# Down weights of an expert in one transfer of 4 MB, and the last expert's in freed up buffers

## The chip, the core and the metric

The kernel runs on one core of a Trainium2 chip. The metric is the device time of one execution in microseconds, lower is better; the median of three runs before the change is 1358.1 us (1355.83 to 1360.45).

## The reference

One block of a hybrid decoder on 256 tokens of width 1024, preceded by 16 meta tokens: a Mamba-2 branch and a latent-attention branch, merged by gates, and after them a mixture of 32 experts of which every token uses four. The change touches the loading of the experts' weights alone. What the experts compute:

```python
logits = (tok_x @ w_router + b_router)            # 256 x 32
top_logit, top_e = lax.top_k(logits, 4)
top_w = softmax(top_logit)
# for every expert e, over the tokens that chose it:
hb = x_pad[tok_blk] @ w1[e] + b1[e]               # 1024 -> 2048, "up"
ob = clamped_swiglu(hb) @ w2[e] + b2[e]           # 1024 -> 1024, "down"
y += ob * w_blk                                   # back to the tokens' rows
out = rms_norm(h + y, norm_final)
```

All weights are float32. An expert has 8 MB of up weights and 4 MB of down weights, so the experts read 384 MB from HBM.

## The kernel before

Every engine has a hand-written instruction stream; nothing is scheduled by a planner. The engines meet through counting semaphores. The first third of the time is the two branches; their weights ("slabs") pass through a ring of six slots of 2 MB. From about 412 us on the same ring and parts of a work area hold expert weights.

**Weights in units.** A unit is 2 MB: 128 partitions with a row of 4096 floats (16 KB) each. An expert has four up units and two down units. There are two sets of up buffers, `w1_sb` for even experts (ring slots 3, 4, 5, 0) and `w1_odd` for odd ones, and one set of down buffers, `w2_sb` (slots 2 and 1). Expert 1's first down half comes early, in two pieces of 1 MB, into `extra`.

**Order of the transfers.** All weight transfers are issued by SyncE (SP), in order, each behind a wait until its buffer is free. An issued transfer joins one queue, which the 16 DMA engines serve in order. `load_up(e, t, odd)` issues four units: the first three wait on `up_used`, which TensorE raises after each of the first three pairs of up matmul steps, the last on `up_done`. `load_down(e, t)` issues the first down unit when TensorE has used half of the expert before (`down_used`, raised after k = 3) and the second when it has used all of it (`down_done`). Through a loop over experts 2 to 21 (`TURN = 11`) each step issues `load_up(e + 3)` and then `load_down(e + 1)`. Behind the loop, for e = 22 to 28, the two are in the other order: `load_down(e + 1)` first, then `load_up(e + 3)`. So the loop ends with the down weights of expert 22 and the code behind it begins with those of expert 23. The end is `load_down(30)` and `load_down(31)`.

**TensorE.** A step handles expert t's end and expert t+1's beginning: `up(t + 1)` (up bias, then eight k of four matmuls; between them transposes of t's activations, the scatter of t-1 and the gather of t+2), then `down(t)` (eight k of two matmuls). `down` waits for the first down unit before k = 0 and for the second before k = 4. A 32-bit matmul stands in the trace as two instructions. The last step has no gather; `down(30)` has transposes between k = 3 and k = 4, and `down(31)` has the scatter of expert 30 there. After it come the last scatter, the final norm and the store.

The semaphore count needed in a wait grows with the number of transfers that were made into a buffer; an overflow round for experts with more than 64 tokens has its own loop and isn't entered with these inputs.

Of the kernel before, what the change touches and what calls it, by code (L numbers as in the profile page):

```python
# [27 lines left out]
P = 128  # L28
D = 1024
# [16 lines left out]
E = 32  # L46
# [28 lines left out]
NSLOT, SLOT = 6, 4096  # L75
# [5 lines left out]
UNIT = 4096  # L81
W1_UNITS, W2_UNITS = 4, 2
E_UNITS = W1_UNITS + W2_UNITS
W1_SLOT = [3, 4, 5, 0]
W2_SLOT = [2, 1]
ODD_AT = [25736, 13824, 20480, 7168]
EXTRA_AT = [0, 11264]

# [14 lines left out]
def meta_ssd_mla_moe(nc, x, meta, slabs, vecs, rows, wts, b1, b2, out):  # L103
    ctx = ExitStack()
    with ctx:
# [17 lines left out]
        ring = sb("ring", NSLOT * SLOT)  # L123
# [92 lines left out]
        actT = w(4096, 512).rearrange("p (j t) -> p j t", j=4)  # L216
# [6 lines left out]
        actT_last = xgT  # L223
# [34 lines left out]
        def sem(name):  # L258
            return ctx.enter_context(nc.semaphore(name))
# [8 lines left out]
        w2_in = [sem(f"w2_in{i}") for i in range(W2_UNITS)]  # L268
        extra_in = [sem(f"extra_in{i}") for i in range(len(EXTRA_AT))]
        up_used, down_used = sem("up_used"), sem("down_used")  # L270
# [34 lines left out]
        down_done, ob_ready, scattered = sem("down_done"), sem("ob_ready"), sem("scattered")  # L305
# [35 lines left out]

        w1_sb = [ring[:, s * SLOT:s * SLOT + UNIT] for s in W1_SLOT]
        w1_odd = [w(at, UNIT) for at in ODD_AT]
        w2_sb = [ring[:, s * SLOT:s * SLOT + UNIT] for s in W2_SLOT]
# [17 lines left out]
        def _(sp):  # L362
# [6 lines left out]
            def unit_of(e, u):  # L369
                return wts[bass.ds((e * E_UNITS + u) * P, P), :]  # L370
# [2 lines left out]
                buf, arrival = (w1_odd, w1_odd_in) if odd else (w1_sb, w1_in)  # L373
                sp.dma_start(buf[u], unit_of(e, u)).then_inc(arrival[u], 16)

            def load_w2(e, c):
                sp.dma_start(w2_sb[c], unit_of(e, W1_UNITS + c)).then_inc(w2_in[c], 16)

            def load_extra(i):
                half = unit_of(1, W1_UNITS)[:, i * (UNIT // 2):(i + 1) * (UNIT // 2)]  # L380
# [36 lines left out]

            def load_down(e, t):

                sp.wait_ge(down_used, t)  # L420
                load_w2(e, 0)
                sp.wait_ge(down_done, t)
                load_w2(e, 1)

            sp.wait_ge(*used["so3"])
            load_w1(0, 3, False)
# [6 lines left out]
            load_w1(1, 2, True)  # L433
            load_extra(1)
            sp.wait_ge(*used["wout0"])
            load_w2(0, 0)
            sp.wait_ge(*used["wout1"])
            load_w2(0, 1)
            sp.wait_ge(xn_ready, 4)
            sp.wait_ge(h1_squared, 4)  # L440
            sp.wait_ge(h1_kept, 1)
# [2 lines left out]
            load_up(2, 2, 0)  # L444
            load_up(3, 3, 1)
            sp.wait_ge(down_done, 1)
            load_w2(1, 1)
            load_w2(2, 0)
            load_up(4, 4, 0)
            sp.wait_ge(down_done, 2)  # L450
            load_w2(2, 1)
            with sp.Fori(1, TURN) as i:
                for odd in (0, 1):
                    e = 2 * i + odd
# [3 lines left out]
                load_down(e + 1, e + 1)  # L458
                load_up(e + 3, e + 3, (e + 1) % 2)
            load_down(E - 2, E - 2)  # L460
            load_down(E - 1, E - 1)
            sp.wait_ge(count_ready, 1)
            cm = sp.value_load(cmax_i[0:1, 0:1], min_val=0, max_val=SEQ)
            with sp.If(cm > SLOTS):
                with sp.Fori(1, SEQ // SLOTS) as r:
# [880 lines left out]
        def _(pe):  # L1346
# [24 lines left out]
            for i in range(6):  # L1371
                b, k0 = ORDER[i // 2], 4 * (i % 2)
                n = BLOCKS[b][1]
# [348 lines left out]
            def up(t, pair, odd, between):  # L1722

                pe.wait_ge(xgT_ready, t + 1)
                weights, arrival = (w1_odd, w1_odd_in) if odd else (w1_sb, w1_in)
                for k in range(KD):
                    between(k)
                    if k % 2 == 0:
                        pe.wait_ge(arrival[k // 2], 16 * (pair + 1))
# [10 lines left out]
            def down(t, to=6, actT=actT, between=None, first=None):  # L1740

                halves = [w2_sb[0][:, 0:UNIT // 2], w2_sb[0][:, UNIT // 2:UNIT], w2_sb[1][:, 0:UNIT // 2], w2_sb[1][:, UNIT // 2:UNIT]]
                if first == 1:
                    halves[0:2] = extra
                pe.wait_ge(actT_ready, t + 1)
                if between is None:
                    pe.wait_ge(scat_ready, t + 1)
                for k in range(KD):
                    if between is not None and k == 4:
                        between()  # L1750
                    if k == 4:
                        pe.wait_ge(w2_in[1], 16 * (t + 1))
                    elif first == 1 and k in (0, 2):
                        pe.wait_ge(extra_in[k // 2], 16)
                    elif k == 0:
                        pe.wait_ge(w2_in[0], 16 if first == 0 else 16 * t)
                    for j in range(2):
                        at = k % 2 * 1024 + j * 512
                        last = mm(bank[to][j * SLOTS:(j + 1) * SLOTS, :], actT[:, k % 4, (k // 4) * SLOTS:(k // 4 + 1) * SLOTS],
                                  halves[k // 2][:, at:at + 512], k == 0, k == KD - 1)  # L1760
                    if k == 3:
                        last.then_inc(down_used, 1)
                last.then_inc(down_done, 1)

            def expert_round(r):
                t0, pair0 = r * E, r * (E // 2)

                def step(t, pair, odd, gathers, scatters, routing, first=None):
                    def between(k):
                        if k == 2:  # L1770
                            act_transposes(t)
                        elif k == 4:
                            if scatters:
                                scatter(t - 1, scat_last if t is t0 else scat)
                            hot_transposes(t)
                            if routing:
                                weights_trans()
                        elif k == 6 and gathers:
                            pe.wait_ge(actT_ready, t + 1)
                            if routing:  # L1780
                                pe.wait_ge(wT_ready, 1)
# [4 lines left out]
                    up(t + 1, pair, odd, between)  # L1786
                    if gathers:
                        gather_trans(t + 2)
                    if routing:
                        down_bias()  # L1790
                    if gathers:
                        down(t, first=first)
                    else:
                        pe.wait_ge(scat_ready, t + 1)
                        down(t, between=lambda: last_transposes(t + 1))

                def first_between(k):
                    if k == 6:
# [2 lines left out]
                def last_transposes(t):  # L1801
                    act_transposes(t)
                    pe.wait_ge(up_read, t + 1)
                    hot_transposes(t, 5)
# [8 lines left out]
                    pe.wait_ge(count_ready, 1)  # L1813
                up_bias(t0)
                gather_trans(t0)
                up(t0, pair0, 0, first_between)
# [15 lines left out]
                down(t0 + E - 1, 4, actT_last, lambda: scatter(t0 + E - 2))  # L1832

            FIRST = 0
            pe.wait_ge(xn_scaled, 2)
# [35 lines left out]
def pack_experts(inp):  # L1871

    import numpy as np
    up = inp["w_mlp1"][0].reshape(E, W1_UNITS, 2, P, 2, 512, 2).transpose(0, 1, 3, 2, 4, 6, 5).reshape(E, W1_UNITS, P, UNIT)
    down = inp["w_mlp2"][0].reshape(E, W2_UNITS, 4, P, D).transpose(0, 1, 3, 2, 4).reshape(E, W2_UNITS, P, UNIT)
    return np.concatenate([up, down], axis=1).reshape(E * E_UNITS * P, UNIT)


# [48 lines left out]
```

## Time and profile before

| | |
|---|---|
| median of 3 runs | 1358.1 us (1355.83 to 1360.45) |
| profiled execution | 1358.35 us, span 1356.6 us |
| granted TensorE clock, mean | 0.997 |
| TensorE busy | 1304.2 us, 96% of the span |
| DMA queue of SP | 460.63 MB in 33424 packets, 81.5% of 16 engines' span |
| chain that ended last | PE 61%, DMA 29%, issue 4% |

The span is what the profiler sees between the first and the last instruction; the profiled execution took 1.75 us more. The share of busy time doesn't say which of TensorE and the DMA engines sets the time: both are at over 90% through the experts. That is read from the stretches in which one of them waits.

### The profile page before, as it was taken

To read this page: it belongs to the slowest core of one execution; us is meant where nothing else is said; L and a number is where in the kernel's file an instruction comes from. 1 tells how busy PE (TensorE), PEld (TensorE's weight loads), DVE (VectorE), ACT (ScalarE), POOL (GpSimd) and SP (SyncE) were. 2 spreads that over 40 slices of the span, in tenths; PEclk is the share of its full clock that TensorE was granted. 3 is DMA by queue.
4 is the path that set the end of the run, shared out by engine and by line. 5 is a ranking of instruction groups with operands and counts; after the bars stand their busy time and mean duration, and the time that the engine had idled before them with its cause. 6 is when DMAs were issued, how large, how long until landed. Compare 5 with 4: busy or idle time off the path is not lost.

```text
span 1356.6 us, 17927 instructions
## 1 busy us (share of the span) xinstructions
PE 1304.2 (96%) x7105; PEld 638.0 (47%) x7105; DVE 459.3 (34%) x1129; ACT 320.4 (24%) x649; POOL 66.7 (5%) x74
## 2 busy tenths in 40 slices
PE   7999999999999999999999999999999999999995
PEld 5858888899974333333333322333333333333331
DVE  4838889988534211112111211111121111211111
ACT  3636767755411111011101101100110010111011
POOL 0000004422103000000000000000000000000000
PEclk9999999999999999999999999999999999999998
DMA  6431334244878999999999999999999999999994
GB/s 238 148 124 64 125 125 168 107 162 187 337 289 323 422 403 426 429 428 430 427 430 427 429 429 428 429 427 430 428 429 429 428 386 424 431 427 429 428 426 164
DMA packets 33763, 461.85 MB, mean 340 GB/s; under 512 B 3808, under 2 KB 3808, under 8 KB 5552
## 3 DMA queue, kind: packets, MB, share of 16 engines
q1 hardware_dynamic: 33424, 460.63, 81.5%
q8 instruction: 34, 0.56, 0.2%
q10 hardware_dynamic: 288, 0.52, 0.1%
q14 instruction: 17, 0.14, 0.0%
HBM read 460.09 MB, written 1.05 MB: 340 GB/s over the span
## 4 chain that ended last, share of the span: by engine, by line
PE 61%; DMA 29%; issue 4%; POOL 3%; DVE 2%; ACT 1%; SPq 0%; POOLq 0%; DVEq 0%; ACTq 0%
PE bank L1348 58%; DMA ring<-wts_dram 29%; POOL work L517 1%; POOL work L514 1%; PE bank L1690 1%; PE bank L1696 1%; DMA ring<-slabs_dram 1%; DVE split L913 0%; PE bank L1712 0%; PE bank L1479 0%; DVE work L847 0%; DVE work L846 0%; DVE work L845 0%; ACT split L559 0%; PE bank L1499 0%
## 5 line engine op out<-in xcount | busy, mean ns | idle before, releaser
L1348 PE MATMUL bank<-ring,work 128*64 128x512 f32 (+5 forms) x2248 | 541.7, 592 | 29.1 <-DMA ring<-wts_dram 28.1
L1348 PE MATMUL bank<-work 128*64 128x512 f32 (+8 forms) x2216 | 434.0, 546 | 3.2 <-DVE work L1267 1.0
L1348 PEld LDWEIGHTS bank<-ring,work 128*64 128x64 f32 (+2 forms) x2248 | 179.1, 142 | 340.4 <-issue 292.9
L1348 PEld LDWEIGHTS bank<-work 128*64 128x64 f32 (+4 forms) x2216 | 146.5, 143 | 258.8 <-issue 246.8
L1348 PE MATMUL bank<-hn_hi,split 128*128 128x256 f32 (+1 forms) x896 | 173.0, 288 | 1.4 <-DVE split L913 1.3
L1296 DVE COPY work<-bank 128x256 f32<-128x256 f32 x31 | 13.2, 425 | 473.8 <-PE bank L1712 473.8
L1348 PEld LDWEIGHTS bank<-hn_hi,split 128*128 128x128 f32 x896 | 141.4, 189 | 3.4 <-issue 1.9
L1348 PE MATMUL bank<-hn_lo,split 128*128 128x256 f32 (+1 forms) x448 | 127.2, 284 | 0.0
L1271 DVE TENSOR_SCALAR work<-bank 128x512 f32<-128x512 f32 x32 | 22.1, 692 | 273.4 <-PE bank L1348 273.4
L913 DVE TENSOR_TENSOR split<-ring,split 128x1024 fp32r<-128x1024 f32 x80 | 100.0, 1253 | 27.1 <-ACT split L559 26.8
L756 ACT ACTIVATE work<-bank 128x512 f32<-128x512 f32 x32 | 19.1, 598 | 328.3 <-PE bank L1348 324.2
L559 ACT ACTIVATE split<-ring 128x1024 fp32r<-128x1024 f32 x80 | 84.1, 1054 | 36.2 <-PE bank L1348 36.0
L1348 PEld LDWEIGHTS bank<-hn_lo,split 128*128 128x128 f32 x448 | 84.4, 188 | 0.2
L776 ACT ACTIVATE work<-bank 128x512 f32<-128x512 f32 x32 | 19.1, 597 | 223.5 <-PE bank L1348 223.5
L771 ACT ACTIVATE work<-bank 128x512 f32<-128x512 f32 x32 | 19.1, 597 | 146.8 <-PE bank L1696 146.8
L1348 PE MATMUL bank<-y_hi,split 128*128 128x256 f32 x256 | 46.2, 283 | 0.0
L760 ACT ACTIVATE work<-bank 128x512 f32<-128x512 f32 x32 | 19.1, 597 | 106.9 <-PE bank L1690 106.9
L1348 PEld LDWEIGHTS bank<-y_hi,split 128*128 128x128 f32 x256 | 40.0, 192 | 0.0
L1348 PE MATMUL bank<-y_lo,split 128*128 128x256 f32 x128 | 36.2, 283 | 0.0
L514 POOL TENSOR_SCALAR work<-work 128x256 f32<-128x256 f32 x16 | 14.1, 884 | 237.5 <-ACT work L701 237.5
L1696 PEld LDWEIGHTS bank<-shifted,work 128*128 128x128 f32 x128 | 13.4, 140 | 26.0 <-issue 26.0
L1690 PEld LDWEIGHTS bank<-shifted,work 128*128 128x128 f32 x128 | 13.4, 140 | 26.0 <-issue 25.2
(247 smaller groups left out, 899.9 us busy)
## 6 DMA issues: line engine op xcount, KB each, us to landing
ring<-wts_dram SPq DMA_DIRECT2D x127, 2048.0 KB, 24.2
work<-wts_dram SPq DMA_DIRECT2D x64, 2048.0 KB, 25.3
ring<-slabs_dram SPq DMA_DIRECT2D x23, 2048.0 KB, 7.5
ring<-slabs_dram SPq DMA_DIRECT2D x2, 1152.0 KB, 5.2
work<-wts_dram SPq DMA_DIRECT2D x2, 1024.0 KB, 19.8
work<-x_dram SPq DMA_DIRECT2D x3, 512.0 KB, 11.5
ring<-slabs_dram SPq DMA_DIRECT2D x1, 1536.0 KB, 12.0
ring<-slabs_dram SPq DMA_DIRECT2D x1, 1280.0 KB, 8.7
```

The lines of the kernel that those rows point to most:

```text
L514: link(pool.tensor_scalar(ztanh[:, c % 2, :], ztanh[:, c % 2, :], 1.0, None, ALU.add))
L517: pool.tensor_tensor(zw, ztanh[:, c % 2, :], zcopy[:, c % 2, :], ALU.mult).then_inc(zw_ready, 1)
L559: a.activation(split[p % NSPLIT][:, 0], piece(p), ACT.Copy).then_inc(hi_ready, 1)
L756: a.activation(xg[:, :], bank[7][:, :], ACT.Copy).then_inc(xg_ready, 1)
L760: a.activation(xgT[:, :, :].rearrange("p j t -> p (j t)"), bank[7][:, :], ACT.Copy).then_inc(xgT_ready, 1)
L771: a.activation(actT[:, :, :].rearrange("p j t -> p (j t)"), bank[7][:, :], ACT.Copy, scale=0.5).then_inc(actT_ready, 1)
L776: a.activation(ob[:, :], bank[at][:, :], ACT.Copy).then_inc(ob_ready, 1)
L913: d.tensor_tensor(split[p % NSPLIT][:, 1], piece(p), split[p % NSPLIT][:, 0], ALU.subtract).then_inc(lo_ready, 1)
L1271: d.tensor_scalar(glu[:, :], bank[4][:, :], LIMIT, None, ALU.min).then_inc(glu_ready, 1)
L1348: return pe.matmul(o, lhsT, rhs, start=start, stop=stop)
L1690: last = pe.transpose(bank[7][:, j * P:(j + 1) * P], xg[:, j * P:(j + 1) * P], ident[:, :])
L1696: last = pe.transpose(bank[7][:, j * P:(j + 1) * P], act[:, j * P:(j + 1) * P], ident[:, :])
```

## The change

The two down units of an expert become one transfer: `w2_sb` is now one buffer of 8192 columns over ring slots 1 and 2, the weights lie in HBM with 32 KB in a row for each partition, and `load_down` waits for `down_done` alone and issues 4 MB. `down_used` is gone. `down` waits for the whole 4 MB before k = 0. Experts 0 and 1 still get halves (expert 0 both, expert 1 the second; its first comes into `extra` as before). Experts 2 to 30, 29 of them, get the 4 MB transfer.

The last expert's down weights don't go to `w2_sb`: its first 2 MB go to `w1_sb[0]` and the rest, as 1 MB, 512 KB and 512 KB, to `w1_sb[1]`. Expert 30's up weights were there, and the waits are for `up_used` of expert 30. `down(31)` waits for the pieces before k = 0, 4, 6 and 7. The order of the loop and of the code behind it is the same as before.

```diff
-W2_SLOT = [2, 1]
+W2_SLOT = 1
...
-            def load_w2(e, c):
-                sp.dma_start(w2_sb[c], unit_of(e, W1_UNITS + c)).then_inc(w2_in[c], 16)
+            wide = wts.rearrange("(a b) n -> a (b n)", b=2)
+            def w2_of(e):
+                return wide[bass.ds((e * (E_UNITS // 2) + W1_UNITS // 2) * P, P), :]
+            def load_w2_half(e, c):
+                sp.dma_start(w2_sb[:, c * UNIT:(c + 1) * UNIT], w2_of(e)[:, c * UNIT:(c + 1) * UNIT]).then_inc(w2_in, 16)
...
             def load_down(e, t):
-                sp.wait_ge(down_used, t)
-                load_w2(e, 0)
                 sp.wait_ge(down_done, t)
-                load_w2(e, 1)
+                sp.dma_start(w2_sb, w2_of(e)).then_inc(w2_in, 16)
...
             sp.wait_ge(down_done, 1)
-            load_w2(1, 1)
-            load_w2(2, 0)
+            load_w2_half(1, 1)
             load_up(4, 4, 0)
-            sp.wait_ge(down_done, 2)
-            load_w2(2, 1)
+            load_down(2, 2)
...
             load_down(E - 2, E - 2)
-            load_down(E - 1, E - 1)
+            sp.wait_ge(up_used, (E - 2) * (W1_UNITS - 1) + 1)
+            sp.dma_start(w1_sb[0], w2_of(E - 1)[:, 0:UNIT]).then_inc(w1_in[0], 16)
+            sp.wait_ge(up_used, (E - 2) * (W1_UNITS - 1) + 2)
+            for at, n, arrival in ((0, 2048, w1_in[1]), (2048, 1024, extra_in[0]), (3072, 1024, extra_in[1])):
+                sp.dma_start(w1_sb[1][:, at:at + n], w2_of(E - 1)[:, UNIT + at:UNIT + at + n]).then_inc(arrival, 16)
...
-                    if k == 4:
-                        pe.wait_ge(w2_in[1], 16 * (t + 1))
+                    if final and k in (0, 4):
+                        pe.wait_ge(w1_in[k // 4], 16 * (E // 2 + 1))
+                    elif final and k >= 6:
+                        pe.wait_ge(extra_in[k - 6], 32)
                     elif first == 1 and k in (0, 2):
                         pe.wait_ge(extra_in[k // 2], 16)
-                    elif k == 0:
-                        pe.wait_ge(w2_in[0], 16 if first == 0 else 16 * t)
+                    elif first == 1 and k == 4:
+                        pe.wait_ge(w2_in, 48)
+                    elif k == 0 and not final:
+                        pe.wait_ge(w2_in, 32 if first == 0 else 16 * (t + 1) if later else 16 * (t + 2))
...
-                    if k == 3:
-                        last.then_inc(down_used, 1)
                 last.then_inc(down_done, 1)
```

On SP, where the loop ends and the code behind it begins (`COMPARE_AND_BRANCH` closes the loop), before:

```order
L377 ISA [waits down_used]
L377 DMA ring<-wts_dram 128x4096
L377 ISA [waits down_done]
L377 DMA ring<-wts_dram 128x4096
L452 REGISTER_ALU
L452 COMPARE_AND_BRANCH
L377 DMA ring<-wts_dram 128x4096 [waits down_used]
L377 DMA ring<-wts_dram 128x4096 [waits down_done]
L374 DMA work<-wts_dram 128x4096 [waits up_used] x3
L374 DMA work<-wts_dram 128x4096 [waits up_done]
```

The same place now:

```order
L426 ISA [waits down_done]
L426 DMA ring<-wts_dram 128x8192
L453 REGISTER_ALU
L453 COMPARE_AND_BRANCH
L426 DMA ring<-wts_dram 128x8192 [waits down_done]
L374 DMA work<-wts_dram 128x4096 [waits up_used] x3
L374 DMA work<-wts_dram 128x4096 [waits up_done]
```

Expert 22's transfer and expert 23's still stand next to each other, and the second now waits for the end of `down(22)` instead of its middle. The end of SP's weights, before:

```order
L374 DMA work<-wts_dram 128x4096 [waits up_done]
L377 DMA ring<-wts_dram 128x4096 [waits down_used]
L377 DMA ring<-wts_dram 128x4096 [waits down_done]
L377 DMA ring<-wts_dram 128x4096 [waits down_used]
L377 DMA ring<-wts_dram 128x4096 [waits down_done]
```

The same place now:

```order
L374 DMA work<-wts_dram 128x4096 [waits up_done]
L426 DMA ring<-wts_dram 128x8192 [waits down_done]
L463 DMA ring<-wts_dram 128x4096 [waits up_used]
L466 DMA ring<-wts_dram 128x2048 [waits up_used]
L466 DMA ring<-wts_dram 128x1024 x2
```

The last expert's pieces no longer wait for `down(30)`.

## Rows read from the trace of the kernel before

**Rows 1.** The page: the span, TensorE, the chain by engine, issues of weights.
```profile
span 1356.6 us, 17927 instructions
PE 1304.2 (96%) x7105; PEld 638.0 (47%) x7105; DVE 459.3 (34%) x1129; ACT 320.4 (24%) x649; POOL 66.7 (5%) x74
...
PE 61%; DMA 29%; issue 4%; POOL 3%; DVE 2%; ACT 1%; SPq 0%; POOLq 0%; DVEq 0%; ACTq 0%
...
ring<-wts_dram SPq DMA_DIRECT2D x127, 2048.0 KB, 24.2
```

**Rows 2.** Windows: stretch, length, busy by engine, TensorE clock, DMA share, GB/s.
```profile
550.00:700.00 150.00, 150.00 (x718) 49.44 (x714) 25.84 (x71) 16.76 (x29) 0.00 (x0) 1.00 1.01 429
700.00:1100.00 400.00, 378.78 (x1784) 123.76 (x1776) 57.34 (x157) 39.11 (x68) 0.00 (x0) 1.00 1.01 428
1100.00:1105.00 5.00, 4.46 (x22) 1.68 (x20) 3.95 (x11) 1.11 (x2) 0.00 (x0) 1.00 0.79 338
1105.00:1110.00 5.00, 3.88 (x22) 1.25 (x24) 0.00 (x0) 0.07 (x1) 0.00 (x0) 1.00 0.80 269
1110.00:1115.00 5.00, 5.00 (x28) 1.50 (x23) 0.00 (x0) 0.53 (x1) 0.00 (x0) 1.00 0.99 400
1115.00:1120.00 5.00, 5.00 (x25) 1.75 (x24) 0.00 (x0) 0.60 (x1) 0.00 (x0) 1.00 1.00 423
1120.00:1290.00 170.00, 170.00 (x808) 56.09 (x806) 26.69 (x73) 17.44 (x30) 0.00 (x0) 1.00 1.01 428
```

**Rows 3.** Chain of waits: start, us, what. A DMA piece runs from issue to landing.
```profile
757.67 25.47 DMA ring<-wts_dram
783.19 3.68 PE bank L1348 x16
787.04 25.48 DMA ring<-wts_dram
...
1080.73 25.45 DMA ring<-wts_dram
1106.23 8.26 PE bank L1348 x40
...
1130.26 11.62 PE bank L1348 x56
...
1157.66 11.62 PE bank L1348 x56
...
1298.28 22.77 DMA ring<-wts_dram
```

**Rows 4.** SP's issues in time: start, us from first to last, count.
```profile
480.31 0.81 SPq L377 DMA_DIRECT2D ring<-wts_dram  x2
484.91 15.52 SPq L374 DMA_DIRECT2D ring<-wts_dram  x4
507.70 0.33 SPq L377 DMA_DIRECT2D ring<-wts_dram  x1
...
1080.73 29.53 SPq L377 DMA_DIRECT2D ring<-wts_dram  x3
```

**Rows 5.** The issue at 500.1 us and its landing.
```profile
L374 SPq DMA_DIRECT2D ring<-wts_dram x1: 328/328/328, 500.1 to 500.1; - x1
...
DMA to landing us min/median/max: 13.6/13.6/13.6
```

**Rows 6.** The issue at 1105.1 us and its landing.
```profile
L377 SPq DMA_DIRECT2D ring<-wts_dram x1: 342/342/342, 1105.1 to 1105.1; - x1
...
DMA to landing us min/median/max: 7.7/7.7/7.7
```

**Rows 7.** DMA packets in 1040 to 1100 us (rows of 16 KB).
```profile
DMA packets 1771, 25.71 MB, mean 428 GB/s; under 512 B 202, under 2 KB 202, under 8 KB 202
...
q1 hardware_dynamic: 1771, 25.71, 100.7%
```

**Rows 8.** DMA packets in 353 to 354.5 us (rows of 8 KB).
```profile
DMA packets 78, 0.64 MB, mean 426 GB/s; under 512 B 1, under 2 KB 1, under 8 KB 1
...
q1 hardware_dynamic: 78, 0.64, 102.1%
```

**Rows 9.** Timeline of TensorE near the end: start, us, what, [idle before].
```profile
1294.58 7.09 PE L1348 MATMUL bank<-ring,work 128*64 128x512 f32 x32
...
1321.19 3.65 PE L1348 MATMUL bank<-ring,work 128*64 128x512 f32 x16 [1.33 <-DMA ring<-wts_dram]
...
1325.96 3.65 PE L1348 MATMUL bank<-ring,work 128*64 128x512 f32 x16 [0.32 <-DMA ring<-wts_dram]
...
1333.16 5.35 PE L1348 MATMUL bank<-ring,work 128*64 128x512 f32 x16 [3.54 <-DMA ring<-wts_dram]
...
1338.44 1.99 PE L1348 MATMUL bank<-work 64*128 64x512 f32 x8
...
1340.36 3.65 PE L1348 MATMUL bank<-ring,work 128*64 128x512 f32 x16
```

**Rows 10.** Windows at the end, columns as in rows 2.
```profile
1330.00:1333.00 3.00, 0.00 (x0) 0.00 (x0) 0.00 (x0) 0.26 (x1) 0.00 (x0) 1.00 0.98 385
1333.00:1338.00 5.00, 4.84 (x16) 1.78 (x16) 0.00 (x0) 0.00 (x0) 0.00 (x0) 0.66 0.78 319
```

More of the change, by code:

```diff
@@ L267, in meta_ssd_mla_moe @@
         w1_odd_in = [sem(f"w1_odd_in{i}") for i in range(W1_UNITS)]
-        w2_in = [sem(f"w2_in{i}") for i in range(W2_UNITS)]
+        w2_in = sem("w2_in")
         extra_in = [sem(f"extra_in{i}") for i in range(len(EXTRA_AT))]
-        up_used, down_used = sem("up_used"), sem("down_used")
+        up_used = sem("up_used")
         pool_step, dve_step, act_step = sem("pool_step"), sem("dve_step"), sem("act_step")
@@ L343, in meta_ssd_mla_moe @@
         w1_odd = [w(at, UNIT) for at in ODD_AT]
-        w2_sb = [ring[:, s * SLOT:s * SLOT + UNIT] for s in W2_SLOT]
+        w2_sb = ring[:, W2_SLOT * SLOT:W2_SLOT * SLOT + 2 * UNIT]
         extra = [w(at, UNIT // 2) for at in EXTRA_AT]
@@ L374, in load_w1 @@
                 sp.dma_start(buf[u], unit_of(e, u)).then_inc(arrival[u], 16)
[L376 to L377 removed]
+            wide = wts.rearrange("(a b) n -> a (b n)", b=2)
[3 more added lines that the diff above has]
+                sp.dma_start(w2_sb[:, c * UNIT:(c + 1) * UNIT], w2_of(e)[:, c * UNIT:(c + 1) * UNIT]).then_inc(w2_in, 16)
             def load_extra(i):
[L380 removed]
+                half = w2_of(1)[:, i * (UNIT // 2):(i + 1) * (UNIT // 2)]
                 sp.dma_start(extra[i], half).then_inc(extra_in[i], 16)
@@ L435, in _ @@
             sp.wait_ge(*used["wout0"])
-            load_w2(0, 0)
+            load_w2_half(0, 1)
             sp.wait_ge(*used["wout1"])
-            load_w2(0, 1)
+            load_w2_half(0, 0)
             sp.wait_ge(xn_ready, 4)
@@ L464, in _ @@
             with sp.If(cm > SLOTS):
+                sp.wait_ge(down_done, E)
                 with sp.Fori(1, SEQ // SLOTS) as r:
@@ L1720, in up_bias, with up @@
                            b1all[i * E:(i + 1) * E, j * 512:(j + 1) * 512], True, False)
-            def up(t, pair, odd, between):
+            def up(t, pair, odd, between, later=False):
                 pe.wait_ge(xgT_ready, t + 1)
@@ L1728, in up @@
                     if k % 2 == 0:
-                        pe.wait_ge(arrival[k // 2], 16 * (pair + 1))
+                        extra_use = 1 if later and not odd and k < 4 else 0
+                        pe.wait_ge(arrival[k // 2], 16 * (pair + 1 + extra_use))
                     for i in range(2):
@@ L1738, in up, with down @@
                 last.then_inc(up_done, 1)
-            def down(t, to=6, actT=actT, between=None, first=None):
-                halves = [w2_sb[0][:, 0:UNIT // 2], w2_sb[0][:, UNIT // 2:UNIT], w2_sb[1][:, 0:UNIT // 2], w2_sb[1][:, UNIT // 2:UNIT]]
+            def down(t, to=6, actT=actT, between=None, first=None, later=False, final=False):
+                halves = [w2_sb[:, i * (UNIT // 2):(i + 1) * (UNIT // 2)] for i in range(4)]
                 if first == 1:
                     halves[0:2] = extra
+                if final:
+                    halves = [w1_sb[0][:, 0:UNIT // 2], w1_sb[0][:, UNIT // 2:UNIT], w1_sb[1][:, 0:UNIT // 2], w1_sb[1][:, UNIT // 2:UNIT]]
                 pe.wait_ge(actT_ready, t + 1)
@@ L1785, in step @@
                     up_bias(t + 1)
-                    up(t + 1, pair, odd, between)
+                    up(t + 1, pair, odd, between, later=r is not FIRST)
                     if gathers:
@@ L1791, in step @@
                     if gathers:
-                        down(t, first=first)
+                        down(t, first=first, later=r is not FIRST)
                     else:
                         pe.wait_ge(scat_ready, t + 1)
-                        down(t, between=lambda: last_transposes(t + 1))
+                        down(t, between=lambda: last_transposes(t + 1), later=r is not FIRST)
                 def first_between(k):
@@ L1815, in expert_round @@
                 gather_trans(t0)
-                up(t0, pair0, 0, first_between)
+                up(t0, pair0, 0, first_between, r is not FIRST)
                 gather_trans(t0 + 1)
@@ L1831, in expert_round @@
                 pe.wait_ge(up_read, t0 + E)
-                down(t0 + E - 1, 4, actT_last, lambda: scatter(t0 + E - 2))
+                down(t0 + E - 1, 4, actT_last, lambda: scatter(t0 + E - 2), later=r is not FIRST, final=r is FIRST)
             FIRST = 0
@@ L1874, in pack_experts @@
     up = inp["w_mlp1"][0].reshape(E, W1_UNITS, 2, P, 2, 512, 2).transpose(0, 1, 3, 2, 4, 6, 5).reshape(E, W1_UNITS, P, UNIT)
-    down = inp["w_mlp2"][0].reshape(E, W2_UNITS, 4, P, D).transpose(0, 1, 3, 2, 4).reshape(E, W2_UNITS, P, UNIT)
+    down = inp["w_mlp2"][0].reshape(E, 8, P, D).transpose(0, 2, 1, 3).reshape(E, W2_UNITS, P, UNIT)
     return np.concatenate([up, down], axis=1).reshape(E * E_UNITS * P, UNIT)
```

## The prediction, made blind

> **What bounds the kernel now.** I read the page first [rows 1]. TensorE is busy 96% of the span, yet 29% of the chain is DMA; both are near their limit, so the share decides nothing. The windows by stage split it [rows 2]. From 550 to 700 us TensorE has no idle time; from 700 to 1100 us it lacks 21 us (400 less 378.78); from 1120 to 1290 us it has none again. The DMA engines move 428 to 429 GB/s in all three. The reader is to see that the queue of weights is the steady side and that TensorE only now and then feels it.
>
> The chain gives both periods [rows 3]. From 757.67 to 787.04 us is one expert while the weights bind: 29.37 us for six units, 4.89 us for 2 MB. From 1130.26 to 1157.66 us is one expert while TensorE binds: 27.40 us. Every expert thus costs the queue 1.97 us more than TensorE. TensorE runs ahead on data loaded earlier until that lead is used up, and then it follows the queue. At the end it follows the queue: the chain there is a transfer issued at 1298.28 us. So the end of the kernel is the time at which the queue has delivered its last units, plus a tail, and any microsecond in which the queue is empty counts in full, if TensorE catches up later. The experts left after a break decide that.
>
> One break stands in the windows [rows 2]. Against 429 GB/s, the four windows from 1100 to 1120 us lose 5 x (1 - 338/429) = 1.06, 1.86, 0.34 and 0.07 us, 3.3 us together. This is where the loop of SP ends: expert 23's first down unit waits there for the middle of `down(22)`, and the freed up buffers stand behind it. The last unit of expert 22 lands at 1080.73 + 25.45 = 1106.2 us, and the next one was issued at 1105.1 us and took 7.7 us to land [rows 3, 6]. A unit itself takes 4.9 us, so an empty queue costs 2.8 us from issue to first effect.
>
> **The change part by part.**
>
> Fewer and longer packets. In 1040 to 1100 us, 1569 data packets (1771 less 202 small ones) take 100.7% of 16 engines for 60 us, 616 ns each for 16 KB [rows 7]. Packets of 8 KB take 24.5/77 = 318 ns [rows 8]. A cost that does not grow with bytes is then 2 x 318 - 616 = 20 ns at most; this is an estimate from two short windows. An engine has 8 such packets less in each of 29 transfers: at 20 ns that is 160 ns each, 4.6 us in all. The other end is 0, if the hardware cuts the 32 KB row in two. I take 2.3 us, the middle: -2.3 (0 to -4.6).
>
> The loading rule of thumb would give far more. The Trainium skill (SBUF — State Buffer, "The DMA setup-cost knee") says that each transfer pays about 2 us that doesn't scale with bytes and that one should use the largest transfer possible. By that the sum would get 29 x 2 = 58 us back. The rows disagree here: the six transfers of an expert take 29.37 us for 12 MB at 429 GB/s, with no room for six such costs; they are paid beside one another in a full queue.
>
> The start. Before, expert 2's down units were issued at 480.7 us (the first) and at 507.70 us (the second) [rows 4]. Now both go at 507.70 us. The last up unit ahead of it was issued at 484.91 + 15.19 = 500.1 us and landed at 513.7 us [rows 4, 5]; with one unit less ahead it lands at 508.8 us. The 4 MB issued at 507.70 us to a nearly empty queue lands at 507.7 + 7.7 + 4.9 = 520.3 us instead of 508.8 + 9.8 = 518.6 us: +1.7 (1 to 3; the upper end adds half of a start again). TensorE doesn't feel it, but the queue is later by that from there on.
>
> The steady loop. The 4 MB is issued at `down_done` and TensorE must have it whole before k = 0. The period is 29.3 us; `down` takes 7.2 us, so the transfer has 22.1 us from issue to landing, of which 9.8 are its own: some 12 us of up units are still ahead of it, and the queue does not run empty. TensorE's two waits per expert become one of 1.9 us. Cost: 0, hidden behind the queue.
>
> Where the loop ends. SP issues expert 22's 4 MB and then waits with expert 23's until `down(22)` has ended, while the four free up buffers stand behind it. The queue ends with expert 22's landing; TensorE then takes 7.1 us for 32 matmul instructions [rows 9] and 0.1 to signal; then come 2.8 us of start and 9.8 us of transfer. Landing to landing is 19.8 us instead of 9.8, a hole of 10.0 us. The 3.3 us of before go: +6.7. If the clock falls during TensorE's wait, `down(22)` is 1.7 us longer. Range 6.2 to 9.
>
> Is the hole paid back? Between it and the landing of expert 30's down weights lie 44 units, 215 us of queue. TensorE needs 7 x 27.40 us to the end of `down(29)` and 18.2 us for the last up (1301.7 to 1319.9 us [rows 9]). The hole delays TensorE's own line by 3.7 us (the end of `down(22)` goes from 1109.9 us, when the third issue of the group at 1080.73 that waits for it goes [rows 4], to 1106.2 + 1.7 - 1.5 + 7.2 = 1113.6 us, 1.5 being the 20 shorter transfers until then); from there it would be ready for `down(30)` at 1113.6 + 191.8 + 18.2 = 1323.6 us. The queue delivers at 1325.9 + 1.7 + 6.7 - 2.3 = 1332.0 us. The queue binds again two experts before the end, so the hole counts in full.
>
> The end. Before, from the landing of expert 30's second unit (1325.9 us) to the end of the last matmul of `down(31)` (1344.0) there are 18.1 us, with a wait of 3.54 us for expert 31's weights and 5.35 us for 16 instructions that otherwise take 3.65 [rows 9]. Now expert 31's pieces lie directly behind expert 30's 4 MB, all landed 9.8 us after it, before TensorE asks for the second. That wait goes. What is late next is `down(30)`: both its halves now stand behind the landing. The tail is 3.65 + 1.2 + 3.65 for it, then 3.65 + 2.0 + 3.65, 17.8 us, and before it TensorE waits 4.1 us (it is ready 7.2 + 18.0 us after the landing of expert 29's, the next lands 29.3 us after it). Idle for 3.54 us before, TensorE had a granted clock of 0.66 over 1333 to 1338 us against 1.00 [rows 10], part of it at 1.2 instead of 2.4 GHz, and lost 1.7 us. I take the same loss: 19.5 against 18.1, +1.4 (-0.3 without it, +3 with a longer one). Removed instructions on SP and TensorE cost nothing: SP waits for buffers all the time.
>
> **Sum.** -2.3 + 1.7 + 6.7 + 1.4 = +7.5 us. The profiled execution goes from 1358.35 to 1365.9 us; it lies 0.25 us above the median, so the forecast is 1358.1 + 7.5 = 1365.6 us. Low ends together: -4.6 + 1.0 + 6.2 - 0.3 = +2.3, 1360.4. High ends, not all at once: about +13, 1371.
>
> **The rivals.**
>
> Wide rows move faster (the other side). If the 4 MB landed in 9.3 instead of 9.8 us, 29 of them would give 14.5 us instead of 2.3: 1353.4 us. The sum turns to zero at 0.26 us more per transfer than I counted, 2.7% of it. For it speaks only that no 32 KB packet is in the trace; against it that the whole cost per packet is 20 of 616 ns. 0.05.
>
> Every transfer pays its start. If the 2.8 us stood in the stream for each, 29 fewer would give 81 us, more than TensorE can follow: its waits after 700 us are 21.2 + 0.5 + 1.1 + 5.2 = 28 us [rows 2, 9], so the time would be 1330 us. A full queue at 4.89 us per unit speaks against it. 0.01. By the Trainium skill's 58 us it would be the same 1330, since that too is more than the waits.
>
> The low ends meet (no clock loss at the end, packets at 20 ns): +2.3 to +4.1, at 1361.5 us, no change that can be measured. 0.13.
>
> Rows are cut in two (the change doesn't do what it says): the 2.3 us don't come, 1367.9 us. For it: nothing in the trace shows a packet over 16 KB. 0.13.
>
> The clock falls in every joined wait of 1.9 us. Waits up to 1.33 us kept it, 3.54 did not [rows 9]. TensorE's period becomes 27.4 + 1.7 = 29.1 us, still under 29.3; only the hole grows: 1367.3 us. 0.10.
>
> **How the numbers follow.** The forecast has the remaining 0.58. A measurement can tell about 0.3%, 4.1 us, so slower begins at 1362.2 us. Slower: 0.58 + 0.13 + 0.10 = 0.81; the same: 0.13; faster: 0.06. The range is 1359.5 to 1371: below are the faster cases, above what several high ends would add.
>
> **What would show it.** The windows around the end of SP's loop: a hole of 10 us in the DMA engines' work, with SP waiting for `down_done` and the issue some 7 us behind the landing. A packet count lower by 29 x 144, and the period of an expert at 29.3 us while the weights bind. One wait of TensorE per expert of about 1.9 us. In the last 35 us no hole in the queue, a wait of about 4 us before `down(30)` and none before `down(31)`. I am wrong if the period falls below 29.1 us, if TensorE never waits after 1120 us, or if the hole is shorter than 8 us.

## The result and the profile after

The changed kernel takes 1365.38 us (median of 5 runs, 1364.91 to 1365.98) against 1358.1 us, now the median of five executions of the kernel before: a ratio of 1.0051, 95% interval 1.0038 to 1.0063. It is slower by 7.3 us where 7.5 were forecast. The profiled execution took 1365.08 us with a span of 1363.3 us, 6.7 us more than before. Five more executions later gave 1364.51 us against 1358.28 us for the kernel before beside them, 6.2 us slower. Medians of the kernel before lie between 1357.4 and 1358.7 us from set to set, so the cost of the change is known to about 1 us: 6 to 7.5 us.

The page of the kernel after, the same lines as in [rows 1]:

```profile
span 1363.3 us, 17847 instructions
PE 1308.6 (96%) x7105; PEld 640.2 (47%) x7105; DVE 459.1 (34%) x1129; ACT 320.3 (23%) x649; POOL 66.6 (5%) x74
...
DMA packets 29875, 461.84 MB, mean 339 GB/s; under 512 B 3376, under 2 KB 3376, under 8 KB 5376
...
PE 58%; DMA 32%; issue 4%; POOL 3%; DVE 2%; ACT 1%; SPq 0%; POOLq 0%; DVEq 0%; ACTq 0%
...
ring<-wts_dram SPq DMA_DIRECT2D x29, 4096.0 KB, 20.9
```

There are 29 transfers of 4 MB, and 3888 packets fewer than the 33763 of before: 29 x 144 less the 288 of two more pieces for the last expert. So the rows of 32 KB are moved in one packet each; had they been cut, only the small packets would be fewer. The trace's records of single packets say the same: 3712 of them, 29 x 128, have 32768 bytes.

The windows that answer to [rows 2] (stretch, length, busy by engine, TensorE clock, DMA share, GB/s):

```profile
700.00:1100.00 400.00, 381.35 (x1776) 124.77 (x1774) 57.27 (x157) 38.99 (x67) 0.00 (x0) 0.98 1.01 430
...
1105.00:1110.00 5.00, 4.89 (x26) 1.77 (x24) 2.57 (x5) 1.12 (x2) 0.00 (x0) 1.00 0.11 46
1110.00:1115.00 5.00, 5.00 (x24) 1.44 (x20) 1.39 (x7) 0.00 (x0) 0.00 (x0) 1.00 0.00 0
1115.00:1120.00 5.00, 5.00 (x29) 1.60 (x28) 0.00 (x0) 0.60 (x1) 0.00 (x0) 1.00 0.85 308
1120.00:1290.00 170.00, 168.40 (x801) 55.50 (x800) 26.23 (x72) 18.05 (x31) 0.00 (x0) 1.00 1.00 429
```

The reader is to see the DMA column: from 1105 to 1115 us the engines move next to nothing, where before they were at 269 and 400 GB/s. TensorE is fully busy over the same 10 us, so a look at TensorE alone would not find the hole. It does wait again before 1290 us (168.40 of 170), which it did not before.

The chain of waits, start, us and what (compare [rows 3]):

```profile
1027.45 21.98 DMA ring<-wts_dram
1049.47 7.11 PE bank L1354 x32
1056.75 21.98 DMA ring<-wts_dram
...
1087.74 20.26 DMA ring<-wts_dram
1108.05 11.69 PE bank L1354 x56
...
1252.16 21.89 DMA ring<-wts_dram
1274.10 7.11 PE bank L1354 x32
1281.23 23.09 DMA ring<-wts_dram
1304.45 8.80 PE bank L1354 x32
1313.26 20.31 DMA ring<-wts_dram
1333.71 3.65 PE bank L1354 x16
```

The period is now 1056.75 - 1027.45 = 29.30 us, with the whole `down` (7.11 us) behind the landing. Less four up units of 4.89 us each, that leaves 9.7 us for a 4 MB transfer in a full queue. From 1252 us on the chain is the queue again.

SP's issues around the end of its loop, and the landing of the issue at 1115.2 us:

```profile
1087.74 27.77 SPq L426 DMA_DIRECT2D ring<-wts_dram  x2
1115.57 2.06 SPq L374 DMA_DIRECT2D work<-wts_dram  x4
...
DMA to landing us min/median/max: 12.4/12.4/12.4
```

Expert 22's 4 MB landed at 1087.74 + 20.26 = 1108.0 us, expert 23's was issued at 1115.2 and landed at 1127.6: 19.6 us from landing to landing, 9.9 more than a 4 MB transfer takes in a full queue (9.7). Before, the two units of expert 23 landed 13.0 us behind expert 22's (the second issued at 1109.9 us, 9.3 us to land).

TensorE at the end (answers to [rows 9]):

```profile
1304.45 8.78 PE L1354 MATMUL bank<-ring,work 128*64 128x512 f32 x32 [2.88 <-DMA ring<-wts_dram]
...
1333.71 3.65 PE L1354 MATMUL bank<-ring,work 128*64 128x512 f32 x16 [2.40 <-DMA ring<-wts_dram]
...
1338.10 7.09 PE L1354 MATMUL bank<-ring,work 128*64 128x512 f32 x32
...
1347.03 3.65 PE L1354 MATMUL bank<-ring,work 128*64 128x512 f32 x16
```

`down(31)` has no wait any more: the second half of `down(30)` and the first of `down(31)` stand in one row of 32 instructions.

### The profile page after: what moved, and what is told of

Its sections match the earlier page's. It is cut to its first block, busy times and chain, and to the rows that moved or that the text cites. A ratio compares the mean times of both kernels' runs of the same rounds, so it can differ in the third digit from the quotient of the medians.

```text
span 1363.3 us, 17847 instructions
## 1 busy us (share of the span) xinstructions
PE 1308.6 (96%) x7105; PEld 640.2 (47%) x7105; DVE 459.1 (34%) x1129; ACT 320.3 (23%) x649; POOL 66.6 (5%) x74
## 4 chain that ended last, share of the span: by engine, by line
PE 58%; DMA 32%; issue 4%; POOL 3%; DVE 2%; ACT 1%; SPq 0%; POOLq 0%; DVEq 0%; ACTq 0%
PE bank L1354 56%; DMA ring<-wts_dram 32%; POOL work L523 1%; POOL work L520 1%; DMA ring<-slabs_dram 1%; PE bank L1696 1%; PE bank L1702 1%; DVE split L919 0%; PE bank L1485 0%; PE bank L1718 0%; DVE work L853 0%; DVE work L852 0%; DVE work L851 0%; ACT split L565 0%; PE bank L1505 0%
## 5 line engine op out<-in xcount | busy, mean ns | idle before, releaser
L919 DVE TENSOR_TENSOR split<-ring,split 128x1024 fp32r<-128x1024 f32 x80 | 100.0, 1252 | 27.1 <-ACT split L565 26.8
```

The costliest lines, as they stand in the source:

```text
L919: d.tensor_tensor(split[p % NSPLIT][:, 1], piece(p), split[p % NSPLIT][:, 0], ALU.subtract).then_inc(lo_ready, 1)
```

## The experiments

All times are medians: of five executions for most kernels, of six for the last expert's weights in the kernel before, of eleven for each of the two kernels with the order turned in three steps, of four for the second run of the 16 KB kernel. Each of the three sets ran beside the kernel before on the same chip, which gave 1358.7, 1357.4 and 1358.3 us. The changed kernel is called "the change" below. It was timed with the result (1365.38 us) and in the third set (1364.51 us), but not in the first two, so a difference to it from these carries about 1 us of doubt between sets.

**Rows of 16 KB in the 4 MB transfer.** One transfer as in the change, but the weights lie in units as before.

```diff
             def w2_of(e):
-                return wide[bass.ds((e * (E_UNITS // 2) + W1_UNITS // 2) * P, P), :]
+                return wts[bass.ds((e * E_UNITS + W1_UNITS) * P, 2 * P), :].rearrange("(c p) n -> p c n", c=2)
...
-                sp.dma_start(w2_sb, w2_of(e)).then_inc(w2_in, 16)
+                sp.dma_start(w2_pair, w2_of(e)).then_inc(w2_in, 16)
```

> The changed kernel with one edit: the down weights lie in HBM in rows of 16 KB again, and the single 4 MB transfer takes two such rows per partition. Same waits, same number of transfers. Theory (the cost is per packet): the 4 MB takes 2 x 4.89 = 9.79 us from landing to landing instead of 9.71, 29 times, +2.3 us on 1365.4, 1367.7. Rival (what was saved came from having fewer transfers and semaphore writes): 1365.4. A second rival (wide rows are read better by HBM, hidden so far behind something): over 1370.

Measured: 1369.81 us, ratio to before 1.0081 (1.0067 to 1.0095), 4.4 us over the change. Two transfers of its chain, with the weights binding:

```profile
1028.47 22.04 DMA ring<-wts_dram
...
1059.54 20.33 DMA ring<-wts_dram
```

They land at 1050.51 and 1079.87 us, 29.36 us apart, which is the period of the kernel before. The number of transfers is that of the change, so the gain in the period (29.30 us) is by packets, and the rival that fewer transfers save something is out. But 4.4 us are more than the packets explain, so it ran again beside the change.

> The changed kernel once more, beside the next two on the same chip: 1365.4, within 0.8.

> The kernel of e1_rows_16k (rows of 16 KB in the 4 MB transfer) again. The first time it was 4.4 us slower than the changed kernel where the packets explain 2.3; its trace has TensorE at half clock for 2.8 us before down(30), behind a wait of 4.21 us. Theory (both belong to it: 2.3 of packets and about 2 of the clock, which falls at another place since the waits are longer): 4 to 4.5 us over the changed kernel. Rival (the clock's part was chance): 2.3 over it.

Measured: the change 1364.51 us, the 16 KB kernel 1370.52 us: 6.0 us apart, more than the theory's 4 to 4.5, and the rival of 2.3 is out. The rows of the first run show where more than 2.3 us come from. Its weights for expert 30 land 1.9 us later than those of the change (1335.5 against 1333.6), which is the packets' part. Then TensorE at the end (timeline) and the windows there:

```profile
1335.64 6.46 PE L1355 MATMUL bank<-ring,work 128*64 128x512 f32 x16 [4.21 <-DMA ring<-wts_dram]
```

```profile
1335.00:1342.00 7.00, 6.36 (x16) 1.91 (x16) 0.01 (x1) 0.00 (x0) 0.00 (x0) 0.55 0.98 413
```

The 16 instructions take 6.46 us instead of 3.65, with a granted clock of 0.55 in the 7 us, mostly at the lower of the two levels (1.2 against 2.4 GHz). That is 2.8 us on the path, 4.7 together. The trace of the second run has the clock fall at two places that count, `down(22)` (chain) and `down(30)` (timeline):

```profile
1108.67 13.38 PE bank L1355 x56
...
1336.73 5.35 PE L1355 MATMUL bank<-ring,work 128*64 128x512 f32 x16 [2.58 <-DMA ring<-wts_dram]
```

The 56 instructions that begin with `down(22)` take 11.69 us in the trace of the change beside it. The 1.7 us more delay the issue of expert 23's weights into an empty queue, and 1.7 us more are lost in `down(30)`; with 2 us of packets that is 5.4 us, and the spans differ by 5.2 (1368.0 and 1362.8 us). Wide rows thus save about 2 us by packets, as forecast. The loss of clock on the path came on top in both traces of the 16 KB kernel, 2.8 and 3.4 us, at different places; why this kernel loses it and the change doesn't is not shown.

**The up units first, the last expert's pieces before expert 30's.**

```diff
+                load_up(e + 3, e + 3, (e + 1) % 2)
                 load_down(e + 1, e + 1)
-                load_up(e + 3, e + 3, (e + 1) % 2)
-            load_down(E - 2, E - 2)
...
+            load_down(E - 2, E - 2)
```

> The changed kernel with the order behind SP's loop as in the loop (the up units of e + 3 first, then the down weights of e + 1) and the last expert's pieces ahead of expert 30's 4 MB. No two down transfers stand next to each other, so the hole of 10 us near 1110 us goes. Theory A, as the prediction put it (each empty microsecond of the queue counts in full): 1355.5. Theory B (the order at the end counts too: the down weights of expert 29 come four units later in the queue, 19.6 us, less the hole of 9.9; from their landing TensorE has 7.2 + 18.2 + 8.4 + 9.3 = 43.1 us of work left, against 17.1 behind expert 30's): landing of expert 29's at 1304.3 + 9.7 = 1314.0, last matmul at 1357.1 instead of 1350.7, 1371.8. I expect B.

Measured: 1370.29 us, ratio 1.0080 (1.0066 to 1.0094), 4.9 us slower than the change though the hole is gone. Theory A falls. TensorE at its end:

```profile
1313.55 7.09 PE L1354 MATMUL bank<-ring,work 128*64 128x512 f32 x32 [0.23 <-DMA ring<-wts_dram]
...
1342.88 7.09 PE L1354 MATMUL bank<-ring,work 128*64 128x512 f32 x32
...
1351.82 3.65 PE L1354 MATMUL bank<-ring,work 128*64 128x512 f32 x16
```

Expert 29's weights come at 1313.4 us instead of 1304.3, and behind them TensorE has no wait until the end of `down(31)` at 1355.5 us, 4.8 us later than in the change. B holds; it put that end at 1357.1 us, 1.6 too late: the landing came 0.6 us earlier, and the work behind it took 42.1 us and not 43.1.

**The hole alone: the order turned in three steps.**

```diff
+                ahead = (2, 2, 2, 1, 1, 1, 0)[e - 2 * TURN]
+                load_up(e + 3, e + 3, (e + 1) % 2, range(ahead))
                 load_down(e + 1, e + 1)
-                load_up(e + 3, e + 3, (e + 1) % 2)
+                load_up(e + 3, e + 3, (e + 1) % 2, range(ahead, W1_UNITS))
```

> The changed kernel with the order of transfers turned in three steps instead of one: behind SP's loop, 2, 2, 2, 1, 1, 1 and 0 of the four up units of e + 3 go ahead of the down weights of e + 1, the rest behind it, so that the end has the same order as before and the queue always has up units in it while SP waits for down_done. Theory (the hole of 9.9 us counts in full when the order at the end stays): expert 30's weights land at 1333.6 - 9.9 = 1323.7, last matmul at 1340.8, 1355.5; up to 2.8 more if the clock falls before down(30). Rival (TensorE binds behind the old hole, so that only its own delay of 3.7 us comes back): 1361.7.

Measured: 1355.08 us, ratio 0.9984 (0.9975 to 0.9993). That is 2.3 us under the kernel before beside it, and 10.3 us under the change. The change ran in other sets; measured each against the kernel before beside it, the two lie 8.5 to 9.6 us apart, and their spans 10.0 to 10.5. The hole's 9.9 us thus come back whole or nearly so, and the rival of 1361.7 us is out. The windows across the old hole, and SP's issues:

```profile
1105.00:1110.00 5.00, 4.87 (x24) 1.76 (x24) 3.95 (x11) 1.11 (x2) 0.00 (x0) 1.00 1.00 426
1110.00:1115.00 5.00, 5.00 (x28) 1.41 (x26) 0.00 (x0) 0.60 (x1) 0.00 (x0) 1.00 1.08 413
1115.00:1120.00 5.00, 5.00 (x26) 1.77 (x24) 0.00 (x0) 0.60 (x1) 0.00 (x0) 1.00 0.92 387
```

```profile
1085.77 0.33 SPq L426 DMA_DIRECT2D ring<-wts_dram  x1
1090.23 4.51 SPq L374 DMA_DIRECT2D work<-wts_dram  x2
1113.22 0.33 SPq L426 DMA_DIRECT2D ring<-wts_dram  x1
```

Expert 23's 4 MB is still issued 7.2 us behind expert 22's landing. The wait of SP is the same; two up units in the queue cover it. So what the merge costs at this place is the hole and not the wait. Behind 1106 us TensorE waits once for weights, before `down(30)`:

```profile
1323.24 3.65 PE L1356 MATMUL bank<-ring,work 128*64 128x512 f32 x16 [0.19 <-DMA ring<-wts_dram]
```

Its own work and the queue thus reach the end nearly together; a queue that is faster still would give no more than that 0.19 us.

**The same with expert 30's weights in two halves.**

```diff
-            load_down(E - 2, E - 2)
+            sp.wait_ge(down_done, E - 2)
+            for c in range(2):
+                sp.dma_start(w2_sb[:, c * UNIT:(c + 1) * UNIT], w2_of(E - 2)[:, c * UNIT:(c + 1) * UNIT]).then_inc(extra_in[c], 16)
```

> As e6_gradual, and expert 30's down weights as two transfers of 2 MB with a wait each, expert 31's as two of 2 MB. Theory: down(30) begins with the first half, 4.9 us earlier, until TensorE's own line binds (43.1 us behind the landing of expert 29's weights at 1294.4: 1337.5 against 1340.8): 1352.2. Rival (the wait before down(30) isn't on the path once the hole is gone): the same as e6_gradual.

Measured: 1355.70 us, ratio 0.9987 (0.9978 to 0.9996), no gain over 1355.08. The rival holds: the wait taken away was only the 0.19 us above, and TensorE's own work of 27.4 us per expert sets the end. My figure of 1337.5 us for TensorE's line began at the landing of expert 29's weights, put at 1294.4 us, but in the trace of the kernel with whole transfers TensorE comes to `down(29)` only at 1297.9 us and finds them there.

**One part of the change alone: the last expert's weights, in the kernel before.** TensorE's waits for them are changed as in the change.

```diff
             load_down(E - 2, E - 2)
-            load_down(E - 1, E - 1)
+            sp.wait_ge(up_used, (E - 2) * (W1_UNITS - 1) + 1)
+            sp.dma_start(w1_sb[0], unit_of(E - 1, W1_UNITS)).then_inc(w1_in[0], 16)
+            sp.wait_ge(up_used, (E - 2) * (W1_UNITS - 1) + 2)
+            for at, n, arrival in ((0, 2048, w1_in[1]), (2048, 1024, extra_in[0]), (3072, 1024, extra_in[1])):
+                sp.dma_start(w1_sb[1][:, at:at + n], unit_of(E - 1, W1_UNITS + 1)[:, at:at + n]).then_inc(arrival, 16)
...
```

> The kernel before with one part of the change alone: expert 31's down weights go into the up buffers of expert 30, in pieces, and don't wait for down(30). Units of 2 MB, two waits and the order stay. Theory: the wait of 3.54 us before down(31) and the 1.7 us at half clock behind it go, and nothing else: 1358.1 - 5.2 = 1352.9. Rival (TensorE meets the weights of expert 30 anyway, so nothing is won, as the tail of the changed kernel with its gain of only 1 us suggests): 1357.

Measured: 1354.94 us, ratio 0.9967 (0.9955 to 0.9979): 3.7 us faster. Its timeline of TensorE:

```profile
1322.02 3.65 PE L1353 MATMUL bank<-ring,work 128*64 128x512 f32 x16 [1.31 <-DMA ring<-wts_dram]
...
1326.82 3.65 PE L1353 MATMUL bank<-ring,work 128*64 128x512 f32 x16 [0.34 <-DMA ring<-wts_dram]
1331.87 3.65 PE L1353 MATMUL bank<-ring,work 128*64 128x512 f32 x16 [1.39 <-DMA ring<-wts_dram]
```

The wait of 3.54 us is not gone but 1.39 us long, since the first piece of 2 MB needs its 4.9 us behind expert 30's unit; the slow stretch behind it is gone. This part of the change is a gain by itself.

**The other part alone: the merge, in the changed kernel.**

```diff
-            sp.wait_ge(up_used, (E - 2) * (W1_UNITS - 1) + 1)
-            sp.dma_start(w1_sb[0], w2_of(E - 1)[:, 0:UNIT]).then_inc(w1_in[0], 16)
...
+            load_down(E - 1, E - 1)
...
```

> The changed kernel without the last part: expert 31's down weights are a 4 MB transfer into the down buffer, issued when down(30) has ended. Theory: issue at 1333.7 + 8.4 = 1342.1, landing 2.8 + 9.8 us later at 1354.8, a wait of 12.6 us and 1.7 us of half clock before down(31), last matmul at 1365.8 instead of 1350.7: +15, 1380.5. Rival (the queue's start is hidden and down(30) ends earlier than I think): +10, 1375.

Measured: 1380.55 us, ratio 1.0160 (1.0146 to 1.0174), 15.2 us over the change. The merge alone costs 21.9 us over the kernel before beside it; most of that is a wait before `down(31)`:

```profile
1353.59 5.47 PE L1350 MATMUL bank<-ring,work 128*64 128x512 f32 x16 [12.58 <-DMA ring<-wts_dram]
```

**Expert 2's weights in halves, in the changed kernel.**

```diff
             load_w2_half(1, 1)
+            sp.dma_start(w2_sb[:, 0:UNIT], w2_of(2)[:, 0:UNIT]).then_inc(early_in, 16)
             load_up(4, 4, 0)
-            load_down(2, 2)
+            sp.wait_ge(down_done, 2)
+            load_w2_half(2, 1)
```

> The changed kernel with expert 2's down weights in two halves as before the change, the first issued when down(1) ... that is when down(0) has ended, the second when down(1) has, and the wait for both before k = 0. Theory: the queue's short break near 510 us goes (measured 2.2 us later than in the kernel before by then) and everything behind it comes earlier by that: 1363.2. Rival (a lead lost so early is bought back before the queue binds): 1365.4.

> The kernel of e8_start (expert 2's down weights in halves) again. Its trace showed the break of 2.3 us at 507 us gone and another of 2.5 us at 535 us in its place, behind the first 4 MB transfer, with 0.5 us left over. Theory: 0.5 us under the changed kernel. Rival (the full 2.2 us): 1363.2.

Measured: 1364.20 us, and 1363.78 us beside 1364.51 for the change: 0.7 us, within the scatter. Two windows, first of the change, then of this kernel:

```profile
510.00:515.00 5.00, 5.00 (x26) 1.76 (x24) 0.00 (x0) 0.60 (x1) 0.00 (x0) 1.00 0.73 315
...
535.00:540.00 5.00, 5.00 (x28) 1.38 (x26) 0.00 (x0) 0.60 (x1) 0.00 (x0) 1.00 1.09 469
```

```profile
510.00:515.00 5.00, 5.00 (x26) 1.77 (x24) 0.00 (x0) 0.60 (x1) 0.00 (x0) 1.00 1.01 426
...
535.00:540.00 5.00, 5.00 (x30) 1.68 (x24) 0.00 (x0) 0.42 (x2) 0.00 (x0) 1.00 0.93 347
```

The break moves from expert 2's 4 MB to expert 3's. In both kernels the first 4 MB that waits for `down_done` meets a nearly empty queue. The start term is a cost of the merge and isn't removed by this one exception.

**A version that beats both.** Units of 2 MB and two waits per expert as before, the last expert's weights in the up buffers in four pieces of 1 MB, and one up unit ahead of the down weights for e = 22 to 24.

```diff
+                ahead = (1, 1, 1, 0, 0, 0, 0)[e - 2 * TURN]
+                load_up(e + 3, e + 3, (e + 1) % 2, range(ahead))
                 load_down(e + 1, e + 1)
...
+            sp.wait_ge(up_used, (E - 2) * (W1_UNITS - 1) + 1)
+            for i, arrival in ((0, w1_in[0]), (1, extra_in[0])):
+                sp.dma_start(w1_sb[0][:, i * 2048:(i + 1) * 2048], unit_of(E - 1, W1_UNITS)[:, i * 2048:(i + 1) * 2048]).then_inc(arrival, 16)
...
```

> The kernel before (2 MB units of 16 KB rows, two waits per expert) with expert 31's down weights in the up buffers of expert 30 as four pieces of 1 MB, and one up unit ahead of the down weights for e = 22 to 24, so that the queue has work while SP waits for the middle of down(22). Theory: 3.9 us for the last expert, as in e4_before_last_only, 1.4 for the shorter first piece (the wait of 1.39 us before down(31) goes), 3.4 for the hole: 1358.7 - 8.7 = 1350.0. Rival (the hole of before is not on the path): 1353.4.

Measured: 1350.80 us, ratio 0.9951 (0.9938 to 0.9965), 6.6 us faster than the kernel before beside it, where the theory gave 8.7. The part for the last expert alone had given 3.7, so the shorter piece and the filled hole together gave some 2.8 (each kernel beside the kernel before of its set) and not 4.8. The timeline of the kernel with that part alone says why: its waits before `down(30)` and `down(31)` are 1.31, 0.34 and 1.39 us, 3.0 together, and behind them TensorE's own work is the limit. The issues around the end of the loop:

```profile
1085.78 0.34 SPq L374 DMA_DIRECT2D work<-wts_dram  x1
1105.75 5.14 SPq L377 DMA_DIRECT2D ring<-wts_dram  x2
```

It beats the change with its hole repaired (1355.08) by 4.3 us, by 3.0 in the spans of the two traces. Both are bound by TensorE behind 1110 us, so what counts is when `down(22)` ends: at 1110.5 us here and at 1113.2 us there, because a whole `down` lies behind the landing of one 4 MB transfer, and half of one behind a unit's. That is 2.7 us of the 3.0; the rest of the 4.3 is not explained.

## Why the prediction was right

The forecast, +7.5 us, and its terms against the two traces (span +6.7):

| Step | forecast, us | measured, us | read from |
|---|---|---|---|
| fewer packets | -2.3 | -2.0 | period 29.30 for 29.37 us, 29 times |
| the start | +1.7 | +2.2 | landing of expert 3's weights, 3.1 us later, less 0.9 by which this execution was late already at 480 us |
| the steady loop | 0 | 0 | the queue at 430 GB/s, one wait of TensorE of 1.83 us per expert |
| the hole | +6.7 | +6.6 | 19.6 us for 13.0 from landing to landing |
| the tail behind expert 30's landing | +1.4 | -1.0 | 17.1 for 18.1 us |

The measured terms sum to 5.8 us, and with the 0.9 us of this execution to 6.7. The start figure in the table comes from 536.2 + 15.2 = 551.4 us against 535.3 + 13.0 = 548.3 us.

The mechanism was right: the hole carries the sum, and it is where it was said to be. That the time came within 0.2 us of the forecast is in part luck. The tail was 2.4 us too high, the start 0.5 too low, and the lateness of 0.9 us at 480 us was in no term. The second trace of the change doesn't have that lateness, and its span is 6.2 us over that of before, 1.3 us under the forecast.

**Fewer packets.** Right, and by packets: the 16 KB kernel loses them again. The rival that rows are cut is out by the count. But the -2.3 us was the middle between rows that are cut (0) and rows that aren't, at 20 ns a packet (-4.6). They aren't cut, and the price was too high: 0.07 us per transfer over 8 packets less per engine is 9 ns. In the trace's records of single packets the median is 613 ns for 16 KB and 1218 ns for 32 KB, so two of the one cost 8 ns more than one of the other. The two errors cancel, and the term's size is luck. By the rule of the Trainium skill (SBUF — State Buffer, "The DMA setup-cost knee") the estimate was 58 us; the trace after shows 29 transfers fewer worth 2.0 us. In a full queue the fixed cost is paid beside the other transfers; it showed up whole only where the queue was empty, as 12.4 us to land for 4 MB that otherwise take 9.7; the kernel with the merge alone shows 12.40 us again, before `down(31)`.

**The hole.** Right in its place, its length and its price, and the three-step order shows that it counts in full or nearly so (8.5 to 10.3 us back, by what it is measured against). The argument that the queue binds again two experts before the end holds too: TensorE's first wait there is at 1274 us. But the sentence that any empty microsecond of the queue counts in full was too wide. It holds only with the order at the end kept, as the kernel with the up units first shows: no hole, and 4.9 us slower. The order decides which work stands behind the last landings.

**The tail.** The mis-sized term. I took a wait of 4.1 us before `down(30)` and 1.7 us of slow clock behind it. Measured: 2.40 us of wait and 3.65 us for the 16 instructions, so no loss; the work behind the landing took 17.1 us where the pieces had been summed to 17.8. These two, 1.7 and 0.7 us, are the term's whole error. The clock fell one expert earlier instead, behind the wait of 2.88 us before `down(29)` (8.78 us for 7.09), and those 1.7 us came out of the next wait, since expert 30's landing did not depend on them.

The windows there, with the clock in the third column from the right:

```profile
1304.00:1309.00 5.00, 4.55 (x14) 1.79 (x16) 0.56 (x2) 0.00 (x0) 0.00 (x0) 0.66 1.03 439
1309.00:1333.00 24.00, 22.31 (x106) 7.22 (x102) 1.97 (x4) 1.82 (x3) 0.00 (x0) 1.00 1.00 428
```

In both traces of the 16 KB kernel the clock did fall before `down(30)`, and the time rose by it. The rival that it falls in every joined wait was half true. Two experts of the change, one after the other:

```profile
1049.47 7.09 PE L1354 MATMUL bank<-ring,work 128*64 128x512 f32 x32 [1.82 <-DMA ring<-wts_dram]
...
1078.77 8.78 PE L1354 MATMUL bank<-ring,work 128*64 128x512 f32 x32 [1.83 <-DMA ring<-wts_dram]
```

Behind the same wait, 4 of the 13 `down` between 700 and 1100 us take 8.8 us and 9 take 7.1 (a mean clock of 0.98 there), and the queue hid the four. At the hole it would not be hidden: the second run of the 16 KB kernel lost 1.7 us there, as the rival said.

**The rivals.** Wide rows move faster: 0.07 us per 4 MB, not the 0.5 it would have taken. That every transfer pays its start is out by the same figure. The low ends did not meet. The two halves of the change have opposite signs: the last expert's part gives 3.7 us by itself, the merge takes it and more.

## What to carry to other kernels

When a transfer queue sets the pace, look for the places where two transfers stand next to each other that each wait for the one consumer: merging or enlarging them there opens a hole of the consumer's work plus the start of a transfer, even if the steady loop doesn't change. The hole is closed by transfers whose buffers are free already, put between the two; how many are needed is the hole's length over a unit's time. In a full queue the larger transfer saved only the fixed part of its packets here, and it makes the consumer start later. A queue made better than TensorE's own pace gives nothing more, as the halves for expert 30 show.

## What the runs showed of the hardware

- A row of 32 KB per partition went as one packet (3712 packets of 32768 bytes; 3888 packets fewer, as counted above), and a 4 MB transfer took 9.7 us from landing to landing where two of 2 MB took 9.8.
- The median packet took 613 ns for 16 KB and 1218 ns for 32 KB.
- From an empty queue 4 MB took 12.4 us to land and 2 MB 7.7 us: 2.7 and 2.8 us of start each. About 1 us of the 2.7 lies ahead of the data: the 4 MB was issued at 1115.2 us, and no byte moved before 1116 us. The rest lies behind the last byte.
- TensorE's clock fell behind waits of 1.83 us in some experts and not in others of the same shape; in the trace before, no wait of up to 1.33 us was followed by a slower stretch. Before `down(30)` it fell behind 2.58 us (second run of the 16 KB kernel) and not behind 2.68 (second run with expert 2's weights in halves). Nor does the loss follow the wait: 1.8 us behind 12.58 us (the merge alone), 1.7 behind 3.54 (the trace before), 3.0 behind 3.19 (second run of the change, before `down(29)`). What decides between them stays open.
